# At three stage boundaries the diagonal scale matrix is written by ScalarE instead of VectorE

## The reference, cut to what matters

```python
def rms_norm(x, g):
    y = x * lax.rsqrt(jnp.mean(x * x, axis=-1, keepdims=True) + RMS_EPS)
    return y * g

# first block
mix = nsa_gmlp_mixer(rms_norm(h, norm_mix_pre), ...)
h = h + rms_norm(mix, norm_mix_post)
ffn = swiglu_ffn(rms_norm(h, norm_ffn_pre), w_gate_up, w_down)
h = h + rms_norm(ffn, norm_ffn_post)
# second block
h = rmsnorm(x, pre_norm_mix) * (1.0 + scale_m) + shift_m
...                                   # sparse attention and a state-space mixer on h
x = x + gate_m * rmsnorm(mix, post_norm_mix)
h2 = rmsnorm(x, pre_norm_ffn) * (1.0 + scale_f) + shift_f
f = (jax.nn.silu(u_gate) * u_up) @ w_ffn_out
x = x + gate_f * rmsnorm(f, post_norm_ffn)
```

## Time and profile before

| | |
|---|---|
| median of 3 runs | 1019.42 us (1017.52 to 1026.19) |
| the profiled execution's own time | 1024.9 us |
| its span in the trace | 1023.2 us |
| mean granted TensorE clock | 0.982 of full speed |
| TensorE busy | 967.9 us (95%) |
| VectorE busy | 669.2 us (65%) |
| ScalarE busy | 544.7 us (53%) |
| GpSimd busy | 292.4 us (29%) |

### The profile page before, as it was taken

The page is one execution under the profiler, slowest core; times in us unless marked ns, Lnnn a source line. Parts: engine busy times, 40 slices in busy tenths (PEclk is TensorE's granted clock), DMA queues, the critical chain, the costliest instruction groups (busy, mean ns, idle before and its releaser), DMA issues.

```text
span 1023.2 us, 16542 instructions
## 1 busy us (share of the span) xinstructions
PE 967.9 (95%) x6146; PEld 844.2 (83%) x6146; DVE 669.2 (65%) x1066; ACT 544.7 (53%) x952; POOL 292.4 (29%) x259
## 2 busy tenths in 40 slices
PE   7998988999998989998999999999989989999997
PEld 6976867888887679798989999997889878888786
DVE  4457566677778656985556756676977477755543
ACT  4367466544543465943446546557764564444443
POOL 3014305111114245598961034340121150000010
PEclk9998999999999999999999999999999999999999
DMA  7665324799989742562107756662235767676572
GB/s 236 187 176 144 125 83 144 246 270 284 287 268 338 221 133 83 145 170 78 43 22 242 222 154 185 173 178 63 83 96 177 242 195 220 212 219 186 170 223 81
DMA packets 141421, 179.12 MB, mean 175 GB/s; under 512 B 7859, under 2 KB 117213, under 8 KB 141346
## 3 DMA queue, kind: packets, MB, share of 16 engines
q1 hardware_dynamic: 130624, 144.53, 45.8%
q0 software_dynamic: 10144, 33.19, 11.0%
q10 hardware_dynamic: 578, 0.41, 0.1%
HBM read 176.98 MB, written 1.12 MB: 174 GB/s over the span
## 4 chain that ended last, share of the span: by engine, by line
PE 81%; DVE 7%; ACT 6%; issue 2%; DMA 2%; POOL 1%; ACTq 0%; DVEq 0%; SPq 0%
PE bank L1901 26%; PE bank L1990 11%; PE bank L1992 11%; PE bank L1991 11%; ACT w_hi L868 1%; PE bank L2028 1%; PE bank L2168 1%; DVE isc L1705 1%; PE bank L2427 1%; PE bank L2423 1%; PE bank L1932 1%; PE bank L2447 1%; DVE w_lo L1318 1%; PE bank L2362 1%; PE bank L2534 1%
## 5 line engine op out<-in xcount | busy, mean ns | idle before, releaser
L1318 DVE TENSOR_TENSOR w_lo<-w_raw,w_hi 128x1024 fp32r<-128x1024 f32 (+1 forms) x227 | 274.4, 1235 | 100.2 <-ACT w_hi L868 93.9
L868 ACT ACTIVATE w_hi<-w_raw 128x1024 fp32r<-128x1024 f32 (+1 forms) x258 | 261.7, 1036 | 131.1 <-PE bank L1992 54.4
L1901 PE MATMUL bank<-h_hi,w_hi 128*128 128x256 f32 x560 | 164.8, 294 | 4.2 <-ACT uq L1195 1.9
L1901 PE MATMUL bank<-h_lo,w_hi 128*128 128x256 f32 x560 | 159.5, 285 | 0.0
L1901 PE MATMUL bank<-h_hi,w_lo 128*128 128x256 f32 x560 | 159.5, 285 | 0.0
L1990 PE MATMUL bank<-w_hi,h_hi 128*128 128x512 f32 x384 | 152.4, 397 | 2.4 <-DVE h_lo L1318 1.9
L1992 PE MATMUL bank<-w_hi,h_lo 128*128 128x512 f32 x384 | 150.3, 391 | 0.0
L1991 PE MATMUL bank<-w_lo,h_hi 128*128 128x512 f32 x384 | 150.1, 391 | 0.0
L700 POOL TENSOR_TENSOR w_lo<-w_raw,w_hi 128x1024 fp32r<-128x1024 f32 (+1 forms) x39 | 85.7, 2198 | 126.7 <-DVE w_lo L1318 86.7
L1901 PEld LDWEIGHTS bank<-h_hi,w_hi 128*128 128x128 f32 x560 | 108.6, 194 | 6.7 <-ACT uq L1195 2.1
L1901 PEld LDWEIGHTS bank<-h_lo,w_hi 128*128 128x128 f32 x560 | 108.5, 194 | 0.0
(11 more groups left out here) (455 smaller groups left out, 1881.5 us busy)
## 6 DMA issues: line engine op xcount, KB each, us to landing
w_raw<-in_w_in SPq DMA_DIRECT2D x84, 512.0 KB, 3.8
ada_raw<-in_ada_w POOLq DMA_DIRECT2D x48, 512.0 KB, 5.6
w_raw<-in_w_gate_up SPq DMA_DIRECT2D x88, 256.0 KB, 5.4
w_raw<-in_w_ffn_in SPq DMA_DIRECT2D x88, 256.0 KB, 3.7
w_raw<-in_w_down SPq DMA_DIRECT2D x22, 512.0 KB, 6.5
w_raw<-in_w_ffn_out SPq DMA_DIRECT2D x22, 512.0 KB, 4.5
w_raw<-in_w_out SPq DMA_DIRECT2D x16, 512.0 KB, 4.4
w_raw<-in_w_o_ssd SPq DMA_DIRECT2D x16, 512.0 KB, 3.4
```

The lines of the kernel that those rows point to most:

```text
L868: act.activation(high(u, n), w_raw[:, u % RING, 0:n], ACT.Copy).then_inc(hi_ready, 1)
L1318: return dve.tensor_tensor(dst, src, hi.bitcast(F32), ALU.subtract)
L1901: ins = pe.matmul(out_b[:, s, :], w[:, kk, c], x[:, k0 + k, :], start=k == 0 and s == 0 and step == 0, stop=k == sum(st.ks) - 1 and s == 1 ...
```

## The change

At the three boundaries VectorE only takes the reciprocal and signals a new semaphore, `x_rstd`. ScalarE, right behind its root of line 930, waits for that signal and writes `diag` with an activation: a copy of the identity whose scale is the reciprocal, one number for each partition. It then signals `diag_ready`, as VectorE did. The first norm at the start of the kernel keeps `rstd_x` as it is. The semaphore `gates_ready`, which nothing used, goes.

```diff
-    gates_act, gates_ready = sem("gates_act"), sem("gates_ready")
+    gates_act, x_rstd = sem("gates_act"), sem("x_rstd")
...
@@ ScalarE, square_x(b, t)
             act.activation(st4[:, t, 8:9], st4[:, t, 6:7], ACT.Sqrt, bias=st4[:, t, 7:8], scale=1.0 / D
                            ).then_inc(x_sd, 1)
+            act.wait_ge(x_rstd, 2 * b + t + 1)
+            act.activation(diag[:, t, :], ident, ACT.Copy, scale=st4[:, t, 9:10]).then_inc(diag_ready, 1)
...
@@ VectorE
+        def root_x(n, t):
+
+            dve.wait_ge(x_sd, 2 * n + t + 1)
+            dve.reciprocal(st4[:, t, 9:10], st4[:, t, 8:9]).then_inc(x_rstd, 1)
+
...
@@ VectorE, boundary(b, bias)
             gain_x(b, 0)
-            rstd_x(b + 1, 0)
+            root_x(b + 1, 0)
             piece_lo(b, 0, 0, bias)
...
             gain_x(b, 1)
-            rstd_x(b + 1, 1)
+            root_x(b + 1, 1)
             for p in range(4):
```

## The result

The changed kernel takes 1018.25 us in the median of 22 runs (1008.85 to 1021.62), the kernel before 1023.36 us in the median of 22 runs beside them (1017.52 to 1027.80). The ratio is 0.995, with a 95% interval of 0.9932 to 0.9968: 5.1 us faster, or 3.3 to 7.0 us. That is inside the 1% that stood for "no change" and clear of zero. The profiled execution took 1020.83 us, its span is 1019.1 us.

A forecast was written before the change was run, and what follows sets the result against it. The prediction took TensorE, busy 967.9 of 1023.2 us, as the bound: 5.0 us of shorter waits plus 1.7 us of clock made 6.7 us, and 1019.42 − 6.7 = 1012.7 us, range 1009.0 to 1019.0 us.

The forecast's parts named there:

- The wait at the diagonal: First tiles of three boundaries: diagonal's 2.19, 1.80 and 2.19 us replaced by a 0.39 us activation, saving 5.0 us.
- What the new wait holds up: ScalarE's queue behind the activation: weight unit v + 3 and the activations' high parts start later, nothing late, 0.3 us to spare.
- The collision on VectorE: Tile 1's x_tok additions may run beside GpSimd's split, costing up to 1.0 us, only if TensorE's turn ran at full clock.
- the activation adds 0.1 us to that: nothing: Second tiles: the diagonal takes 0.29 us and TensorE comes 1.2 us later, so a 0.1 us longer activation costs nothing.
- TensorE's clock: Behind the first and third boundaries' gaps: one low-clock stretch fewer, 1.7 us, with 0 and 3.4 us as ends.
- the two losses of 1.7 us: Low clock behind the 3.67 and 3.94 us gaps of the first and third boundaries, costing 1.7 us each.
- The level: Whole kernel: the 6.7 us gain taken from the 1019.42 us median rather than the profiled 1024.9 us, giving 1012.7 us.
- The eaten gain: Rival: behind the first boundary TensorE meets late weights, leaving 3.2 us of gain, 1016.2 us; chance 9%.
- No effect: Rival: reading SBUF beside GpSimd stretches the activation to 2.2 us too, nothing gained, 1019.4 to 1020 us; chance 4%.
- Slower by the clock: Rival: shifted work behind 169 us causes more low-clock stretches at 1.7 us each, a fifth giving 1021.1 us; chance 5%.

The follow-up runs named there:

- both experiments on the kernel before: Kernel before, once with GpSimd's second weight splits waiting for tile 0's diagonal (one execution 1018.64 us), once with VectorE's tensor_scalar also writing its accumulator (1017.29 us, ratio 0.9944).
- the repetition of the change: The changed kernel as it is, run again beside the kernel before: 1017.78 us in 12 runs, ratio 0.9977.
- the kernel before with the shorter filling: Kernel before plus 13 unused identity matmuls, instead of 26, ahead of TensorE's first-tile wait at the first and third boundaries: 1019.93 us, ratio 0.9969.
- the accumulating form: Kernel before, diagonal still on VectorE, its tensor_scalar also adding 0 and writing out its accumulator: 1017.29 us in 10 runs, ratio 0.9944.
- ten places: The change plus 2 to 11 unused identity matmuls in each filled TensorE gap, each filling shorter than its gap: 1010.11 us in 6 runs, ratio 0.9871 to before.

## Why the prediction was right or wrong

**The wait at the diagonal: right.** The forecast read the 2.19 us mostly as waiting for GpSimd; both experiments on the kernel before show it. The activation was put at 0.39 us and took 0.40 us. The saving at the gaps was put at 1.80, 1.41 and 1.80 us, 5.0 us together, and is 1.78, 1.15 and 1.81 us, 4.7 us in all; in three other profiles the middle gap is 0.20 to 0.28 us, which is the forecast 1.4 us. The wait at line 2028 was to fall to about 4.2 us and fell to 4.5 us. The split of the 2.19 us into 1.9 us of waiting and 0.29 us of work was less exact. By the trace GpSimd's first split takes 2.79, 2.40 and 2.79 us at the three boundaries, and the diagonal ends 0.1 us behind it each time, so only that much of its work is left by then.

**What the new wait holds up: right.** The high part of unit `v + 3` comes behind the activation, at 167.70 us, and GpSimd's pair of splits takes 5.32 us instead of 5.28 us; TensorE waits for neither. One small point was wrong: the first split was read as 2.64 us and the second as perhaps delayed by the diagonal. Without that diagonal the pair is no shorter, and its first split alone takes 2.81 us. It overlaps the end of VectorE's gains.

**The collision on VectorE: right, and it costs a little.** For tile 1 the additions to `x_tok` took 2.00 us instead of 1.42 us at the first boundary, for which the forecast gave up to 1.0 us, "only if TensorE has run the turn at full clock". In the profile after the clock fell in the turn, and TensorE came to tile 1 no later for it (8.92 us behind tile 0, before 8.94 us). In the repetition of the change the clock held, and the chain that ended last went through them:

```profile
172.63 2.03 DVE x_tok L1388 x2
```

There TensorE came to tile 1 after 7.67 us, where the kernel before with the shorter filling, its diagonals slow and its clock full, needed 7.32 us. So up to 0.35 us of the 1.78 us is given back at this boundary. With the activation for tile 0 only it was 7.56 us: "the activation adds 0.1 us to that: nothing" holds only where TensorE is late for other reasons.

**TensorE's clock: too large.** The forecast was "one low stretch fewer, 1.7 us". In the profile after there was indeed one fewer at these two places, and in the five executions with gaps of 1.84 to 1.89 and 2.11 to 2.13 us there the clock fell behind two of the ten. But the low-clock time of whole runs did not fall by as much as that saves: it is 24.8 and 25.8 us in the two sets of the change, 23.8 us with the accumulating form, and 25.7 and 27.9 us in the two sets of before. In single profiles other places fall instead (345 to 360 us has a granted clock of 0.89 in the profile after and 1.00 before); that this is where the saving goes in general is not shown. Nor is a low stretch worth 1.7 us everywhere: behind the gap at 429.90 us it costs nothing, and over the 22 runs of the change, the one with the clock at 0.998 took 1008.85 us and the profiled one with 0.983 took 1020.83 us, 12.0 us for 2 × 0.015 × 1015 = 30 us at the low clock, 0.4 us for each.

An estimate of the two parts comes from straight lines of one slope through the 53 runs of before in the later sets and the 44 runs of the change and of the accumulating form: 0.36 us for each us at the low clock, and 3.9 us (3.3 to 4.4) between the kernels at equal low-clock time. On average those kernels have 1.7 us less of it, which is 0.6 us. So of the 4.7 us of shorter waits about 3.9 us reach the end, and the clock gives some 0.6 us instead of 1.7 us. For the 22 runs of before beside the measured 5.1 us no clock is on record, so its share there stays open. Where the two gaps are filled, some 3 us come back, about the two losses of 1.7 us that the forecast named; the profiles of these kernels have the full clock behind both.

**The level: the step that failed.** The step is the base of the last subtraction. The forecast took the difference "from the median: 1019.42 − 6.7 = 1012.7 us". That median was of three runs, which spread over 8.7 us, and it lay 3.9 us below what the kernel takes: 1023.36 us in 22 runs, and 1022.73 and 1022.79 us in the later sets of 32 and 21. Against 1023.36 us the same difference gives 1016.7 us, 1.6 us from the measured 1018.25 us. So 3.9 us of the miss of 5.5 us are the base, and 1.6 us the difference, 6.7 us where 5.1 us was measured: the clock's 1.7 us was too large, and part of the 5.0 us of waits did not reach the end. The warning was in the text: the profiled execution's 1024.9 us was set aside, and was in fact nearer to the true middle. The 1018.2 us that the forecast wrote down from it and then dropped meets the measured time, but by luck: a base 1.5 us too high and a difference 1.6 us too large cancel. Seen from 1019.42 us, the measured time is a gain of only 1.2 us where 6.7 us was forecast, and it lies near the upper end of the range; counted from 1023.36 us the same range would have it in the middle.

**The rivals.** The eaten gain: not in the form that was forecast; no new gap came behind the first boundary. What is given back is the 0.35 us at tile 1 and whatever else stands between 4.7 and 3.9 us, which no run takes apart. No effect: out, by the six activations of 0.40 us. Slower by the clock: its mechanism is real, as the spread of the runs shows, but it did not turn the sign.

## What to carry to other kernels

When one instruction lasts several times as long as its twin on the same shape, look at what the other engines run at that moment before moving it: here GpSimd held it up. Another form of the same instruction or another engine cured it equally; a wait on the other side cured it too, but moved GpSimd's work into the way of something else. A gap ahead of a matmul can cost twice, once as a wait and once as a slower clock behind it, unless another engine sets the pace there. Filling ten such gaps with matmuls that nobody needs, a little shorter than the gap, was worth more than the change itself; a filling 2.1 us too long at two gaps ate its own gain. And a forecast of a time needs a base from more than three runs when these spread further than the effect: state the difference first, and the level with its own error.

## What was unexpected of the hardware

The filling matmuls recovered 2.9 us in the kernel before, and 7.7 us on top of the change with ten places (from 1017.78 to 1010.11 us, medians of two sets). The clock fell behind a gap of 1.89 us and held behind 2.13 us in the same execution, and behind the gap of 1.85 to 1.89 us at about 430 us it fell in seven executions and held in four. So a gap of this size decides nothing by its length alone. VectorE's plain tensor_scalar of 128x128 took 0.29 us alone and up to 2.19 us beside GpSimd's split, its accumulating form 0.35 us and 0.08 us for the accumulator in either case.
